# Second recurrence: masked products and merges in one stage, the turning to token order inside the first

## The reference, cut to what matters

```python
def step(state, inp):
    r_t, w_t, k_t, v_t, a_t, b_t = inp
    sa = jnp.einsum('bhij,bhj->bhi', state, a_t)
    state = (state * w_t[:, :, None, :] + sa[..., None] * b_t[:, :, None, :]
             + v_t[..., None] * k_t[:, :, None, :])
    return state, jnp.einsum('bhij,bhj->bhi', state, r_t)
```

## Time and profile before

| what | value |
|---|---|
| median of three runs | 3504.23 us (3503.64 to 3510.71) |
| profiled execution, own time | 3512.69 us |
| its span | 3510.9 us |
| granted TensorE clock, mean | 0.972 |
| PE busy | 3348.1 us, 95% |
| DVE busy | 1899.4 us, 54% |
| ACT busy | 1194.1 us, 34% |
| second recurrence, first layer | 592.6 to 745.6 us |
| second recurrence, second layer | 1899.9 to 2046.9 us |

### The profile page before, as it was taken

How to read it: one execution, slowest core, us unless ns; L and a number is a source line. 1 busy time by engine, 2 the same in 40 slices (tenths; PEclk the granted TensorE clock), 3 DMA queues, 4 the chain that set the end, 5 groups by cost and what they waited for, 6 DMA issues and landing times. The chain is left out here.

```text
span 3510.9 us, 49199 instructions
## 1 busy us (share of the span) xinstructions
PE 3348.1 (95%) x21362; PEld 2751.4 (78%) x21362; DVE 1899.4 (54%) x2663; ACT 1194.1 (34%) x1676; POOL 8.3 (0%) x8
## 2 busy tenths in 40 slices
PE   7999998799999999999998799999999989999998
PEld 5888887678788888888876778788887858878886
DVE  4434565745454345434675655453446776457475
ACT  3323343133332233223453033332233274344242
POOL 0000000000000000000000000000000000000000
PEclk9999998889999999999998899999999999999999
DMA  3323222013123232323221024123223203323232
GB/s 122 106 88 110 78 81 94 3 55 133 57 96 107 90 102 90 104 89 110 75 79 43 3 68 132 62 96 102 96 97 120 93 5 114 103 73 104 89 103 71
DMA packets 78198, 301.70 MB, mean 86 GB/s; under 512 B 8946, under 2 KB 9586, under 8 KB 77344
## 3 DMA queue, kind: packets, MB, share of 16 engines
q1 hardware_dynamic: 77984, 298.56, 25.5%
HBM read 296.40 MB, written 6.06 MB: 86 GB/s over the span
## 5 line engine op out<-in xcount | busy, mean ns | idle before, releaser
L323 DVE TENSOR_TENSOR w_lo<-ring,w_hi 128x1024 fp32r<-128x1024 f32 (+1 forms) x508 | 652.6, 1286 | 507.4 <-ACT w_hi L316 507.0
L341 PE MATMUL ps<-xa_hi,w_hi 128*128 128x512 f32 x1728 | 689.4, 399 | 16.4 <-DVE w_lo L323 12.6
L342 PE MATMUL ps<-xa_lo,w_hi 128*128 128x512 f32 x1728 | 678.5, 393 | 0.0
L343 PE MATMUL ps<-xa_hi,w_lo 128*128 128x512 f32 x1728 | 678.4, 393 | 0.0
L316 ACT ACTIVATE w_hi<-ring 128x1024 fp32r<-128x1024 f32 (+1 forms) x508 | 555.2, 1099 | 345.2 <-DMA ring<-in_ffn_in_dram 73.5
L341 PE MATMUL ps<-xb_hi,w_hi 128*128 128x512 f32 x1248 | 490.1, 393 | 0.0
L343 PE MATMUL ps<-xb_hi,w_lo 128*128 128x512 f32 x1248 | 486.4, 390 | 0.0
L342 PE MATMUL ps<-xb_lo,w_hi 128*128 128x512 f32 x1248 | 486.3, 390 | 0.0
L341 PEld LDWEIGHTS ps<-xa_hi,w_hi 128*128 128x128 f32 x1728 | 327.9, 190 | 100.4 <-DVE w_lo L323 14.2
L342 PEld LDWEIGHTS ps<-xa_lo,w_hi 128*128 128x128 f32 x1728 | 327.9, 190 | 68.5 <-issue 2.7
L343 PEld LDWEIGHTS ps<-xa_hi,w_lo 128*128 128x128 f32 x1728 | 327.4, 189 | 69.1
(11 more groups left out here) (361 smaller groups left out, 3437.0 us busy)
## 6 DMA issues: line engine op xcount, KB each, us to landing
ring<-in_ffn_in_dram SPq DMA_DIRECT2D x176, 512.0 KB, 3.4
ring<-in_ffn_out_dram SPq DMA_DIRECT2D x64, 704.0 KB, 4.0
ring<-in_mix_in_dram SPq DMA_DIRECT2D x58, 512.0 KB, 3.5
ring<-in_up_dram SPq DMA_DIRECT2D x44, 512.0 KB, 3.4
ring<-in_w_in_dram SPq DMA_DIRECT2D x22, 512.0 KB, 3.5
ring<-in_down_dram SPq DMA_DIRECT2D x16, 704.0 KB, 4.1
ring<-in_mix_out_dram SPq DMA_DIRECT2D x16, 512.0 KB, 4.2
ring<-in_xk_dram SPq DMA_DIRECT2D x16, 512.0 KB, 3.5
```

What stands on the lines that cost most here:

```text
L323: dve.tensor_tensor(core.w_lo[j][:, 0:width], core.ring[j][:, 0:width], core.w_hi[j][:, 0:width].bitcast(F32), ALU.subtract).then_inc(self ...
L341: pe.matmul(out, hi, x_hi, start=(opens and k == tiles[0]), stop=False)
L342: pe.matmul(out, hi, x_lo, start=False, stop=False)
L343: last = pe.matmul(out, lo, x_hi, start=False, stop=(closes and k == tiles[-1]))
```

## The change

Stage (b) goes away as a stage. Its transposes are issued by PE at the end of (a), in the order v, a-hat, b-hat, k-hat, through five banks (`TURN_BANKS`); all 16 copies are ACT's. DVE's order in (a) is changed so that a-hat, b-hat and k-hat come before the decay copy, the bonus product and r-hat, and some links between them fall away.

Stages (c) and (d) become one. Only the products with b-hat are made first. N is made once b-hat's masks of the first four banks are done, and N's transpose by a second set of 48 matmuls. The starts of inv and inv_t are filled with the identity by ACT and overwritten by predicated copies. The products with k-hat are made in eight pieces (`with_k`), two in each of the first four merge rounds. For odd heads inv_t and x lie in the other partition half than before, so that x and the update of inv run on all four quarters; the update of inv_t still takes two, but for the last round, where all four are used and odd heads' inv_t is carried across by products with the identity. DVE's merge instructions cover 128 partitions, in groups of 8 and 4 systems. Buffers are renumbered; stage (e) is otherwise unchanged.

```diff
+TURN_BANKS = (6, 7, 0, 1, 2)
...
+            dve.wait_ge(grown, 2)
+            for m in range(3):
+                dve.scalar_tensor_tensor(ar[:, 0, m], chunks(kk)[:, m], -1.0, chunks(e_prev)[:, m], ALU.mult,
+                                         ALU.mult).then_inc(a_made, 1)
+            link(dve.tensor_tensor(b_hat, kk, gate_a, ALU.mult))
+            dve.tensor_tensor(b_hat, b_hat, e_out, ALU.mult).then_inc(b_made, 1)
+
+            dve.wait_ge(o_gated, 3)
+            dve.tensor_tensor(k_hat, k, e_out, ALU.mult).then_inc(k_made, 1)
...
+            pe.wait_ge(opened, 6)
+            for n, (src, _, ready, count) in enumerate(turns):
+                for q in range(4):
+                    t = 4 * n + q
+                    if t == 2:
+                        pe.wait_ge(a_made, 3)
+                    if q == 0 and ready is not None:
+                        pe.wait_ge(ready, count)
+                    if t >= len(TURN_BANKS):
+                        pe.wait_ge(turned_out, t - len(TURN_BANKS) + 1)
+                    for m in range(3):
+                        last = pe.transpose(ps[:, TURN_BANKS[t % len(TURN_BANKS)], m * P:(m + 1) * P],
+                                            three(src)[:, m, q * P:(q + 1) * P], core.c("ident"))
+                    last.then_inc(turned, 1)
...
+            for t in range(16):
+                act.wait_ge(turned, t + 1)
+                act.activation(turns[t // 4][1][:, t % 4, :], ps[:, TURN_BANKS[t % len(TURN_BANKS)], 0:384],
+                               ACT.Copy).then_inc(turned_out, 1)
...
+        groups, parts_t = ((0, 8), (8, 12)), ((0, 16), (16, 24))
+        n_of = lambda h, r, n12: n_t[half(r), col(h, n12)]
+        x_of = lambda x, h, r, n12: x[half(r ^ h), col(r, n12)]
+        inv_of = lambda h, r, n12: inv[half(r), col(h ^ r, n12)]
+        inv_t_of = lambda h, r, n12: inv_t[half(r ^ h), col(h, n12)]
...
+            def with_k(n):
+                q, h = divmod(n, 2)
+                bank = base(n // 2) + 3
+                for m in range(3):
+                    for r in range(2):
+                        last = pe.matmul(ps[half(r), bank, 128 * m:128 * (m + 1)], chunks(k_hat)[half(h), m, 2 * q + r, :],
+                                         ar[half(h), :, m, 2 * q + r], start=True, stop=True)
+                last.then_inc(made_k, 1)
...
+                    for n12 in range(lo, hi):
+                        for h, r in ((0, 0), (0, 1), (1, 0), (1, 1)):
+                            bank, cols = beside(here, r, n12)
+                            last = pe.matmul(ps[half(r ^ h), bank, cols], n_of(h, r, n12), inv_of(h, r, n12), start=True, stop=True)
+                    last.then_inc(made_x, 1)
...
+                    for g, (lo, hi) in enumerate(groups):
+                        pe.wait_ge(took_x, 2 * n + g + 1)
+                        for n12 in range(lo, hi):
+                            for h, r in ((0, 0), (0, 1), (1, 1), (1, 0)):
+                                bank, cols = beside(there, h ^ r, n12)
+                                last = pe.matmul(ps[half(r), bank, cols], inv_t_of(h, r, n12), x_of(x, h, r, n12), start=True,
+                                                 stop=True)
+                        last.then_inc(made_v, 1)
+                    with_k(2 * n)
+                    for lo, hi in parts_t:
+                        for n24 in range(lo, hi):
+                            h, n12 = divmod(n24, 12)
+                            bank, cols = at(here, n24)
+                            for r in range(2):
+                                last = pe.matmul(ps[half(r ^ h), bank, cols], x_of(x, h, r, n12), inv_t_of(h, r, n12), start=True,
+                                                 stop=True)
+                        last.then_inc(made_tt, 1)
+                    pe.wait_ge(masked_k, 4 * n + 2)
+                    with_k(2 * n + 1)
...
+                dve.copy_predicated(both(inv, g), mask, two_banks(0, g)).then_inc(inverse, 1)
```

More of the change, by code:

```diff
@@ L1934, in vector_all @@
         self.o.vector_all(dve)
[L1937 to L1969, removed]
 def half(h):
@@ L2118, in _ @@
             link(dve.tensor_copy(dec.rearrange("p (m c) -> p m c", m=3), e4[:, :, :, C - 1]))
+            dve.wait_ge(bonus_sum, 1)
+            link(dve.tensor_tensor(three(bonus), three(v), ps[:, 3:6, :], ALU.mult))
             for m in range(3):
                 link(dve.tensor_tensor(ar[:, 1, m], chunks(r)[:, m], e4[:, m], ALU.mult))
[L2121 to L2129, removed]
         @block.tensor
@@ L2194, in rwkv @@
     many = lambda mask, n, k=None: mask.unsqueeze(1).unsqueeze(1).to_broadcast([P, n, k or 24 // n, C])
-    with stage(nc, "made", "masked", "inverse", "step") as (block, made, masked, inverse, step):
+    sizes = LEVELS[1:]
+    n_merge = len(sizes)
+    xs = [a[6], a[7]]
+    with stage(nc, "made", "masked", "made_i", "inverse", "made_it", "inverse_t", "eyed", "blank", "made_x", "took_x",
+               "made_v", "took_v", "made_tt", "took_tt", "made_k", "masked_k") as (
+            block, made, masked, made_i, inverse, made_it, inverse_t, eyed, blank, made_x, took_x, made_v, took_v, made_tt,
+            took_tt, made_k, masked_k):
@@ L2201, in _ @@
+        row = lambda bank, lo, hi: ps[:, bank + lo // 8:bank + (hi + 7) // 8, :].rearrange("p b t -> p (b t)")[:, 0:(hi - lo) * C]
+        of_head = lambda t, h: t[:, h * U3 // 2:(h + 1) * U3 // 2]
+        cut = lambda a, side, size: a.rearrange("p r n (k s t) -> p r n k s t", s=2, t=size)[:, :, :, :, side]
+        columns = lambda t, side, size: t.rearrange("p (k s t) -> p k s t", s=2, t=size)[:, :, side]
         @block.tensor
         def _(pe):
-            for n, lhs in enumerate((b_hat, k_hat)):
-                for q in range(NCH // 2):
-                    if n:
[L2206 to L2245, removed]
@@ L2250, in rwkv @@
[L2250 to L2265, removed]
-                    for r in range(2):
[L2267 to L2278, removed]
-                products(pe, 0, 0, n_t, inv, made_x)
-                if n:
-                    pe.wait_ge(took_tt, 4 * n)
-                products(pe, 1, 1, n_t, inv, made_x)
-                pe.wait_ge(blank, n + 1)
-                pe.wait_ge(took_x, 4 * n + 2)
-                if more:
-                    products(pe, 0, 0, inv_t, x, made_t)
-                    pe.wait_ge(took_x, 4 * n + 4)
-                    products(pe, 0, 1, x, inv_t, made_tt)
-                    pe.wait_ge(took_t, 4 * n + 2)
-                    products(pe, 1, 0, inv_t, x, made_t)
-                    pe.wait_ge(took_tt, 4 * n + 2)
-                    products(pe, 1, 1, x, inv_t, made_tt)
-                else:
-                    products(pe, 0, 0, x, inv_t, made_tt)
-                    pe.wait_ge(took_x, 4 * n + 4)
-                    products(pe, 1, 1, x, inv_t, made_tt)
@@ new lines, in with_k @@
+            def with_k(n):
[6 more added lines that the diff above has]
+                last.then_inc(made_k, 1)
+            for q in range(NCH // 2):
+                for m in range(3):
+                    for h, r in CORNERS:
+                        c = 2 * q + r
+                        last = pe.matmul(ps[half(r), 2 * q + h, 128 * m:128 * (m + 1)], chunks(b_hat)[half(h), m, c, :],
+                                         ar[half(h), :, m, c], start=True, stop=True)
+                last.then_inc(made, 1)
@@ new lines, in _ @@
+            pe.wait_ge(masked, 4)
+            for n12 in range(12):
+                q, m = divmod(n12, 3)
+                for h, r in CORNERS:
+                    bank, cols = beside(0, h ^ r, n12)
+                    last = pe.matmul(ps[half(r), bank, cols], ar[half(h), 0, m, 2 * q + r], chunks(b_hat)[half(h), m, 2 * q + r, :],
+                                     start=True, stop=True)
+            last.then_inc(made_i, 1)
+            pe.wait_ge(masked, 8)
+            for n12 in range(12):
+                q, m = divmod(n12, 3)
+                for h, r in CORNERS:
+                    bank, cols = at(4 + 2 * h, n12)
+                    last = pe.matmul(ps[half(r ^ h), bank, cols], chunks(b_hat)[half(h), m, 2 * q + r, :],
+                                     ar[half(h), 0, m, 2 * q + r], start=True, stop=True)
@@ L2298, in _ @@
         @block.scalar
         def _(act):
+            for buf in (inv, inv_t):
+                act.activation(buf.rearrange("p (n t) -> p n t", t=C),
+                               core.c("eye").unsqueeze(1).to_broadcast([P, U3 // C, C]), ACT.Copy).then_inc(eyed, 1)
             for n, size in enumerate(sizes):
@@ new lines, in _ @@
+            for q in range(NCH // 2):
+                dve.wait_ge(made, q + 1)
+                dve.tensor_tensor(pair_of(n_t, q), made_pair(0, q), many(core.c("before"), 2, 3), ALU.mult).then_inc(masked, 1)
+                dve.tensor_tensor(pair_of(rb, q), made_pair(1, q), many(core.c("upto"), 2, 3), ALU.mult).then_inc(masked, 1)
+            dve.wait_ge(made_i, 1)
```

(4 more changed lines are left out.)

105 lines of the change are left out of this document (79 added, 26 removed).

## The result

The changed kernel took 3465.61 us (median of four runs, 3456.52 to 3467.37), the kernel before, on the same chip, 3506.3 us (four runs, 3503.64 to 3510.71). The ratio is 0.9881, with a 95% interval of 0.9866 to 0.9896. The gain is 40.7 us; 41.4 had been forecast, and a time of 3463 in a range of 3456 to 3468. The profiled execution took 3467.37 us, its span is 3465.3 us and its mean clock 0.981.

What follows compares the result with a forecast made beforehand. Each barrier-separated stage of the second recurrence was taken as bound by its slowest chain, the united stage by PE's instruction fetching. 2 x (10.5 + 10.2) = 41.4 us off the 3504.23 median gave 3463, range 3456 to 3468.

Steps and rivals of the forecast that it cites:

- (b): Second recurrence's turning to token order, 11.1 us; PE makes 48 transposes at the half clock, 8.2 us.
- (a): Second recurrence's preparation, 36.7 us, with DVE busy 31.5 of it and PE done early.
- (c): Second recurrence's masked products, 17.7 us, with PE busy only 7.9 of it.
- (d): Second recurrence's merges, 44.8 us; PE is the limit, busy all of each 8.64 us round.
- (e): Second recurrence's solve and state chain, 42.7 us, 36.4 in the second layer; forecast the same, +-1 us.
- Turning: Transposes and ACT copies move into (a), hidden under DVE, so the next stage starts earlier: -10.5 us a layer.
- Rival 4: Turning is not hidden, by ACT alone or half clock: 2.3 us a layer, 3468; chance 0.23 together with Rival 2.
- Pauses: In the united stage PE gets at most 256 instructions in about 3.6 us, making merge rounds 9.0 us.
- rival 1: Instruction fetching doesn't bind the united stage: rounds of 8.0 us, stage 46.5, total 3453; chance 0.13.
- The stage's terms: United products and merges: 17.3 + 27.0 + 6.1 + 1.1, and 0.8 to the next stage: 52.3 us for 62.5, -10.2.
- Rival 2: Clock falls for part of the united stage as PE pauses: 3468 to 3480; chance 0.23 together with Rival 4.
- Rival 3: Clock stays at half throughout the united stage: 72 us in place of 62.5, total 3515, slower; chance 0.03.

Runs made afterwards that it cites:

- wide_records: Changed kernel with half as many instructions in x and the update of inv, each of 128 columns, values differing from the reference; 3443.82 us in one run.
- two_quarters: Changed kernel with x and the update of inv reordered to use two array quarters at a time, same instructions; 3461.62 us in one run, 3463.54 us timed again.
- stage_only: Kernel before with only the united stage of products and merges new, preparation and turning as before; 3487.78 us, ratio 0.9941 to the kernel before.
- changed_again: The changed kernel unaltered, timed again beside the repeated two_quarters; 3465.15 us over four runs, ratio 0.9878 to the kernel before.
- e5_streams: Changed kernel plus three matmul streams without waits behind the first layer's united stage; 512 matmuls took 27.9 us on four quarters, 30.0 on two.

## Why the prediction was right, and where it was not

*Turning*, -10.5 us a layer: it gave 10.8. DVE set the end of (a), ACT was done 0.9 us before it, and PE transposed at full clock. Rival 4 is out. What the sum left out is that the stage behind the turning then opens at half clock.

*Pauses*: rival 1 (fetching doesn't bind, rounds of 8.0) is out. The first three rounds were 9.7, 9.3 and 9.1 us with pauses some 256 instructions apart. The streams show them without any other work, wide_records takes them away by fewer instructions, and two_quarters shows that the array's speed isn't what sets the round. The size of 3.6 us a block was right for one execution (3.61) and 7% low for the one profiled first (3.85).

*The stage's terms*, forecast 52.3 us. The opening and first round were 18.0 (17.3 forecast): the half clock at the start was not forecast, and stage_only's opening without it was 0.75 us shorter. The next three rounds took 29.7 (27.0 forecast): 0.3 and 0.1 in the first two, 2.3 in the third, of which about 1.5 is the half clock (92 loads in 4.41 us against 2.86) and the rest the block that came after 4.47 us. The k pieces cost what was forecast: a piece's 12 loads in the second round start at 652.25 and end at 652.88, 0.63 us (0.64 forecast). The last round and the way out took 6.3 (8.0 forecast): here the moves through the identity were mis-sized; I had 2.6 us for them, and from 678.06 to 679.17, when the last of their loads ends, they take 1.1, mixed with the final products. The stage came to 54.0 and, in the second layer, to 52.5. Over the eight times that this stage was profiled unaltered (also 50.1 and 52.9 in changed_again, 51.0 and 50.7 in stage_only, 50.0 and 54.3 in e5_streams) the mean is 51.9.

*Rival 2*, the clock for part of the stage, came about for 3 us at each opening and 3.4 us in one round. It cost some 1.5 us where it struck in a round, and 0.75 us at the first layer's opening by the comparison with stage_only. The half clock at the opening is not rival 2's mechanism: it came with PE's 3.5 us of idling behind the transposes, before the stage began. By the Trainium skill ("TensorE: Matmul & The Clock Gate", Part 4), transposes don't count as busy. Two rows speak against that, the first from the kernel before, the second from the changed kernel:

```profile
626.00:630.40 4.40, 0.00 (x0) 0.00 (x0) 3.23 (x2) 0.00 (x0) 0.00 (x0) 0.50 0.00 0
619.90:628.00 8.10, 5.49 (x49) 5.13 (x47) 7.50 (x8) 6.24 (x16) 0.00 (x0) 1.00 0.00 0
```

Before, PE's last sums ended at 621.2, it idled, and from 626.0 on the clock was at half. In the changed kernel nothing but transposes ran from 619.9 to 625.4, and the clock stayed full until 628.0. The earlier trace rows also had the clock rise while PE did nothing but transpose.

*Rival 3*, half clock throughout, is out: 0.94 and 0.97 over the stage.

*(e)*, forecast +-1: it was 7.5 shorter in one layer and 5.6 longer in the other, both with the clock. These two nearly cancel in this pair of profiles. In changed_again's profile (e) was at 0.80 in both layers and took about 40 and 41.7 us, while the first layer's stage ahead of it was 3.9 us shorter. Swings of this size could make up the 12 us between single executions of the unaltered changed kernel (3455.56 to 3467.52); the fastest were not profiled, so that is not shown. What decides in which layer the clock stays low was not found out. That the medians fit to 0.7 us (the profiled execution was forecast at 3471.3 and took 3467.37) owes something to luck: the stage gave 1.9 us less than forecast over both layers, the turning 0.6 more, (e) 2.0 more, and 3.5 came from outside the recurrence. In the medians such differences are within the spread.

## What to carry to other kernels

Where PE runs many small matmuls, count instructions as well as array time: here 256 for PE in 3.6 to 3.85 us on average, 28 to 30 ns for a load and its matmul. Work spread over four quarters (15 to 18 ns a load) passes that rate at once, so a new order over the array gained nothing, while fewer and wider matmuls do (44.6 against 50 to 54 us). The gains that held came from elsewhere: a stage moved under a longer engine, and, by the account of the stages, idle time of PE and a barrier taken out.

## What was not expected of the hardware

- A stream of matmuls with no waits reached 193 loads before its first pause and then stood 1.5 to 2.05 us at each 256th instruction, 3.45 to 4.01 us apart. The Trainium skill ("Runtime: NRT & Kernel Launch", Instruction fetch mechanics) has the cost of such a boundary as mostly hidden; here it is 12 of 28 us.
- The rate isn't constant: blocks of the one stream came 3.45 to 4.01 us apart at full clock, and in the merges one left PE standing for 2.27 us. For that one the packet itself came late: the DMA view has it at 668.9, 2.1 us after PE resumed at 666.87, where the block before had 1.1; from there PE resumed after 2.4 us, as in the streams. What delays a packet was not found out.
- The eight moves through the identity, of 256 and 512 columns, took 1.1 us where the row of 128 columns had suggested 2.6. They may overlap on the two quarters and with the products behind them; that wasn't tried by itself.
